# Natural feature order for the normalised activations of the expert stage: strided weight loads on TensorE in place of a strided write on VectorE

## The reference

```python
h2 = rmsnorm(x, norm2_g[l])
x = x + hier_moe(h2, w_rg[l], b_rg[l], w_re[l], b_re[l], w_eg[l], w_eu[l], w_ed[l])

def hier_moe(h, ...):          # 32 experts, D = 1024, hidden 512
    lg = (t @ w_rg) + b_rg     # group logits, 4
    le = einsum('nd,dge->nge', t, w_re) + b_re
    # one group, two experts in it, softmax weights -> gates (256 x 32)
    for e in range(N_EXPERTS):
        hid = silu(t @ w_eg[e]) * (t @ w_eu[e])
        out = out + gates[:, e:e + 1] * (hid @ w_ed[e])
```

## Time and profile before

| | us |
|---|---|
| median of 3 runs | 1888.01 |
| lowest and highest of them | 1887.04, 1891.11 |
| profiled execution, its own time | 1890.07 |
| its span, first to last instruction | 1887.9 |
| mean granted clock of TensorE | 0.988 |

### The profile page before, as it was taken

One profiled execution on the slowest core, in us unless ns is written; L12 is line 12 of the kernel. 1 busy time (PEld: TensorE's weight loads), 2 busy tenths in 40 slices (PEclk: granted clock), 3 DMA queues, 4 the chain that ended last, 5 costly groups with the idle time before them and its releaser, 6 DMA issues.

```text
span 1887.9 us, 25726 instructions
## 1 busy us (share of the span) xinstructions
PE 1818.1 (96%) x10350; PEld 1399.9 (74%) x10350; DVE 946.1 (50%) x1185; ACT 722.8 (38%) x941; POOL 42.3 (2%) x55
## 2 busy tenths in 40 slices
PE   9988999999999989999989999989999999999997
PEld 8876644544544468888987888778888999888886
DVE  5474311111111146657685656756566654665665
ACT  4443111111111144445564434654245445453444
POOL 2000000000000000000000000000000000200000
PEclk9988999999999999999999999999999999999999
DMA  9523789999999965555424555536555544555551
GB/s 279 160 90 120 322 342 422 422 422 421 422 422 422 422 223 187 191 180 168 157 90 148 181 191 187 183 131 196 180 193 167 179 155 148 165 188 185 185 193 56
DMA packets 191810, 429.43 MB, mean 227 GB/s; under 512 B 7796, under 2 KB 146132, under 8 KB 167168
## 3 DMA queue, kind: packets, MB, share of 16 engines
q1 hardware_dynamic: 187952, 418.41, 60.9%
q0 software_dynamic: 3792, 10.08, 2.0%
HBM read 426.62 MB, written 1.84 MB: 227 GB/s over the span
## 4 chain that ended last, share of the span: by engine, by line
PE 78%; DMA 9%; DVE 7%; ACT 4%; issue 1%; SPq 0%; DVEq 0%; POOL 0%; ACTq 0%
PE pw L488 55%; PE acc L488 22%; DMA mring<-in_w_eu 8%; DVE wl L1596 1%; DMA raw<-in_w_in 1%; ACT arena L1319 1%; PE pw L789 1%; ACT wh L1134 0%; DVE x L2018 0%; ACT sm L1311 0%; ACT arena L1386 0%; DVE scr L2030 0%; ACT L1164 0%; ACT arena L1405 0%; DVE scr L2086 0%
## 5 line engine op out<-in xcount | busy, mean ns | idle before, releaser
L488 PE MATMUL pw<-aa,wh 128*128 128x512 f32 (+1 forms) x2512 | 700.2, 349 | 5.1 <-DVE aa L1624 3.3
L488 PE MATMUL pw<-aa,wl 128*128 128x256 f32 x1960 | 551.7, 281 | 0.0
L1596 DVE TENSOR_TENSOR wl<-raw,wh 128x2048 fp32r<-128x2048 f32 x205 | 463.5, 2298 | 167.7 <-ACT wh L1134 166.4
L488 PEld LDWEIGHTS pw<-aa,wh 128*128 128x128 f32 x2512 | 436.8, 190 | 73.4 <-DVE wl L1596 4.8
L1134 ACT ACTIVATE wh<-raw 128x2048 fp32r<-128x2048 f32 x205 | 381.5, 1905 | 37.5 <-DMA raw<-in_w_in 19.3
L488 PEld LDWEIGHTS pw<-aa,wl 128*128 128x128 f32 x1960 | 372.0, 190 | 1.5
L488 PE MATMUL acc<-wh,aa 128*128 128x512 f32 x1088 | 350.1, 396 | 12.5 <-DVE aa L1622 4.0
L488 PE MATMUL pw<-mring,arena 128*64 128x512 f32 x1536 | 338.5, 595 | 8.4 <-DMA mring<-in_w_eu 7.6
L488 PEld LDWEIGHTS pw<-mring,arena 128*64 128x64 f32 x1536 | 108.8, 137 | 211.4 <-issue 207.8
L488 PEld LDWEIGHTS acc<-wh,aa 128*128 128x128 f32 x1088 | 206.2, 190 | 60.1 <-DVE aa L1622 4.5
L488 PE MATMUL acc<-wl,aa 128*128 128x512 f32 x544 | 213.5, 392 | 0.0
(11 more groups left out here) (387 smaller groups left out, 1344.2 us busy)
## 6 DMA issues: line engine op xcount, KB each, us to landing
raw<-in_ffn_w_in SPq DMA_DIRECT2D x88, 1024.0 KB, 5.1
mring<-in_w_eg SPq DMA_DIRECT2D x64, 1024.0 KB, 18.2
mring<-in_w_eu SPq DMA_DIRECT2D x64, 1024.0 KB, 20.1
mring<-in_w_ed SPq DMA_DIRECT2D x64, 1024.0 KB, 18.8
raw<-in_ffn_w_out SPq DMA_DIRECT2D x44, 1024.0 KB, 5.0
raw<-in_odd_w_in SPq DMA_DIRECT2D x24, 1024.0 KB, 5.2
raw<-in_w_in SPq DMA_DIRECT2D x12, 1024.0 KB, 12.7
raw<-in_even_w_in SPq DMA_DIRECT2D x11, 1024.0 KB, 5.3
```

The lines of the kernel that those rows point to most:

```text
L488: return pe.matmul(out, lhs, rhs, start=start, stop=stop, skip_group_check=True)
L1596: dve.tensor_tensor(wl[:, u % RING, :], raw[:, u % RING, :], wh[:, u % RING, :].bitcast(F32), ALU.subtract).then_inc(sig(f"{ep}_lo"), 1)
```

## The change

`h2` is stored in the order (t, f, k), which is feature order. The VectorE instructions at L1850 then write in one run. Every read of `h2` on TensorE, the transposes of `turn_tokens` and the matmuls of `gather`, loads its 128 columns eight floats (32 bytes) apart. No instruction is added, removed or moved on any engine, and no semaphore changes.

```diff
@@ -191,7 +191,7 @@
         wr = arena[:, 3080:3368].rearrange("p (c g) -> p c g", g=36)
         br = arena[:, 3368:3404]
         rt = arena[:, 3404:4096]
-        h2 = arena[:, 4096:6144].rearrange("p (t k f) -> p t k f", t=NT, k=KC)
+        h2 = arena[:, 4096:6144].rearrange("p (t f k) -> p t k f", t=NT, k=KC)
         h2T = arena[:, 6144:8192].rearrange("p (c t) -> p c t", c=KC)
         masks = rt[:, 264:328].rearrange("p (t e) -> p t e", t=NT)
         silu_s = arena[:, 8192:8448].rearrange("p (c s) -> p c s", c=4)
```

## The result

The changed kernel takes 1948.64 us (median of 4 runs, 1948.01 to 1951.01) and the kernel before 1889.56 us (4 runs, 1887.04 to 1892.18). The ratio is 1.0318, with an interval of 1.0305 to 1.0332. Predicted were 1942.5 us, slower with a chance of 0.69.

A forecast was written before the change was run, and what follows sets the result against it. TensorE bounds the expert stage, with the weight DMA close behind. Terms: -0.65 (write) + 62.8 (gathers) + 1.5 (transposes) - 9.2 (DMA waits) = +54.45 us, 1942.5 us against the median; own range 1934 to 1953, overall 1886 to 1953.

The forecast's parts named there:

- Two limits close together: Expert stage: TensorE limits at 28.24 us a pair, the weight DMA at 29.83; 9.2 us of DMA loss would vanish.
- A weight load that becomes slower therefore costs nothing until the pair is longer than 29.83 us.: Expert stage: slower loads are hidden by 1.59 us of slack for each pair; everything beyond it costs time.
- Rival 1: TensorE loads: stride costs as little as at L789, step at most 118.5 ns, 1887.7 us, not slower; chance 0.29.
- The write: VectorE at L1850: one run saves 1.35 us there, but only 0.65 us of TensorE idle time reaches the end.
- A quarter of which is under 60 ns: Gathers: from 0.23 us per 128x512 matmul, a 128-column matmul takes under 60 ns, so the load sets the step.
- The price of a load: Gather loads at a stride of eight: step of 228 ns instead of 112.5, 115.5 ns more for each load.
- Row (a): Transposes at L789, loading at a stride of four floats: step 118 ns and not 106, taken as nearest TensorE evidence.
- The two lanes: Load reads: assumed two lanes or ports; as later tested, interleaved 16-byte lanes, each access in one some 1.85 ns.
- The stretch to 250 ns for a full DMA: Top of the forecast's load-step range: 250 ns would give 1954 us with the transposes' share.
- Gathers: Expert-stage gather matmuls: 544 loads at 115.5 ns more each, all on the chain, +62.8 us.
- Transposes: The 16 transposes of L578: at 228 ns a load, their last copy ends at 4.29 us, not 2.77; +1.5 us.
- Rival 3: Expert stage: TensorE's clock falls to 0.92, 45 us longer on top of the forecast, 1987 us; chance 0.02.

The follow-up runs named there:

- the two-copy kernel: Against the kernel before: a feature-order copy of h2 written first for the transposes, the old-order copy behind it for the gathers; 1889.30 us against 1888.80, ratio 0.9999.

## Why the prediction was right, point by point

- *Two limits close together.* Right: with the longer pair no wait on the DMA is left, and the 9.2 us read off the chain are what vanishes. The kernels with strides of 4, 8 and 16 fit it within 1 us.
- *"A weight load that becomes slower therefore costs nothing until the pair is longer than 29.83 us."* Wrong. The kernel that adds 0.89 us to a pair stays at 29.14 us and is 9.4 us slower. What is free is 9.2 us over the whole stage, some 0.66 us a pair or 20 ns a load. Rival 1 would have turned slower from a step of about 132 ns on, not 162. The forecast used the total, so its sum was not touched.
- *The write.* -0.65 us, capped by the filler: the two-copy kernel shows the start of the transposes moving by 0.67 us. VectorE itself saved 1.47 us for the 1.35 us worked out.
- *"A quarter of which is under 60 ns", so the load alone sets the step.* Wrong. The row of 0.23 us is that of the scatter, whose operands are fp32r. A plain matmul of 512 moving columns takes 429 ns, a quarter of which is 107, and with only 32 stationary columns the step is still 109 ns. Matmul and load took the same time in the gathers before. The forecast needed only that nothing hides a step of 228 ns, and that held.
- *The price of a load.* 228 ns (219 to 236) for 237 measured. The rows of VectorE, 1.70 and 1.73 ns for an access, were good neighbours: TensorE pays 1.82 and 1.85 at strides of 4 and 8, though 1.70 at 16 and 2.08 at 12. Nothing in the runs says why two engines should pay alike, and TensorE's transposes don't, so the closeness was in part luck. Row (a), the transposes at L789, was read as the same kind of load and is not: had it been the only row, rival 1 would have looked safe. The two lanes that joined (a) with the others were a wrong picture that gave 236 ns by chance (2 x 118); a stride of 16 bytes already costs 232 ns. The stretch to 250 ns for a full DMA wasn't needed: the step is 237 ns beside a DMA at 0.94 and beside one at 0.00.
- *Gathers.* 62.8 us in the forecast; 544 x (237.2 - 111.5) = 68.4 us measured. This term is the one that was sized too small. Measured against its own kernel before, the change cost 59.1 us for a forecast of 54.45; the gathers are +5.6 of the difference, and the transposes go the other way. In the profiled executions the stretch from the first gather to the last copy grew by 59.0 us, and 68.4 - 9.2 is 59.2. Another 1.55 us of the 6.1 by which the time was missed are the kernel before itself, whose median was 1889.56 us beside the changed one and 1888.01 in the forecast.
- *Transposes.* +1.5 us in the forecast. From the first load at 190.64 us to the router's first matmul at 193.63 is 2.99 us, 2.81 before, and the step rose by 13 ns. But that first load now runs beside the last filler. From the end of the filler, 191.03 us, it is 2.60 us, so on the chain the transposes cost nothing. They were priced as plain loads.
- *Rival 3.* The clock stayed at 1.00 in the stage. Ahead of it the granted clock was 0.84 (0.92 before), the router's matmuls took 5.11 us (3.94 before) and the filler behind them 8.81 us (8.35). Whether that is the change's is open: the kernels with strides of 2 and 16 show 0.84 and 5.43 and 5.03 us, those with a stride of 4 and with two copies 0.92 and 3.76 us, each in one profiled execution. It is worth 1.6 us and was in no term of the forecast.
- *The sums.* They come out as written, except that the range of 1934 to 1953 us doesn't quite match its own rows: its lowest step, 219 ns, gives 1937.5 us and its highest, 250 ns, 1954.
- *The Trainium skill.* Its page "SBUF — State Buffer", section "Door 1: The DMA port swizzle", was right that crossing to a new 16-byte line is what costs, and the line count fits 1.8 ns; its "4 fp32" for free is not what a plain load shows (232 ns at four, 173 at three, 118 at two). The Trainium skill's "TensorE: Matmul & The Clock Gate", section "LDWEIGHTS (loading the stationary operand)", which counts columns alone, holds here for contiguous loads and roughly for transposes (109 to 125 ns), not for the gathers.

## What to carry to other kernels

Keep the columns of a stationary or plain moving operand in shared 16-byte lines where a chain of narrow float32 matmuls is bounded by its loads; a stride of two is nearly free, one of four or more doubles the step. Widths matter for a moving operand of fp32r: 128 strided columns are hidden, 256 take 216 to 231 ns for 119. A strided write on another engine that is done once is cheap against strided reads that are repeated (3.95 us once against 68 us over 17 gathers), and a strided load is free where a wide enough matmul stands in front of it (512 plain columns here). Where two limits lie close together, read the slack as one total over the stage, since a stock loaded ahead is eaten up pair by pair.

## What the runs showed of the hardware that was not expected

- A transpose's load at any stride steps at 109 to 125 ns, a plain or fp32r load of the same 128 columns from a stride of 4 on at 217 to 267. fp32r moving operands of 128 columns are cheap as well (112 to 118 ns), and with 256 columns they pay 0.84 to 0.90 ns for a line, half the price; plain ones of 128 are not cheap (217 to 233). The cause is open.
- On the plateau the price is not flat: 266.5 ns at a stride of 12, 250.7 at 24, 217.5 at 16. In the whole kernel 16 was faster than 8 by 11 us.
- A strided load costs about the same at half the granted clock (266 and 222 ns at strides of 12 and 16, against 266.5 and 217.5 at the full one), and the same beside a DMA at a share of 0.94 as beside an idle one (237 ns).
